# Three of eight chunk pairs of twelve projection blocks by seven block products

## The chip, the cores and the metric

The kernel runs on one core of a Trainium2 chip. Its time is the device time of one execution in microseconds, the median of several runs.

## The reference

The reference is a model of one parallel block (stick-breaking attention and chunked attention with relative positions, a gated feed-forward part) and two more layers with state-space, convolution, latent and memory attention parts, in float32, for 256 tokens of width 2048. What matters here is its first projection, of which the first 6144 columns are q, k and v of both attentions:

```
h = rmsnorm(x, g_mix[i])
proj = h @ w_in[i]          # (256, 2048) @ (2048, 10240)
q_sb, k_sb, v_sb, q_ca, k_ca, v_ca, gate_sb, gate_ca = jnp.split(proj, splits, axis=-1)
```

The kernel multiplies by the gain `g_mix` ahead of the product and by the token's `rstd` behind it.

## The kernel before

**Units.** All weights come as one stream of 919 units. A unit is 256 rows (two chunks of 128) by 512 columns of a weight matrix, 128x1024 float32 in SBUF, 512 KB. A block of the projection is 512 columns, thus 8 units (2048 rows). The tokens are two halves of 128 (`TH`). The stage `win` has 20 blocks; the first twelve (6144 columns) are run in a loop of six pairs of blocks, the other eight in a second loop with the attention beside them.

**Three products for one.** Each operand is split into a high part (`w_hi`, rounded to fp32r by ScalarE, line 1287) and a low part (`w_lo` = raw - `w_hi`, by VectorE, line 1883). The sources stand in SBUF as `x_t` in two parts. `unit` (from line 843) does 2 chunks x 2 halves x 3 products = 12 matmuls of 128x128 by 512 columns: eight with `w_hi` (line 853), then, behind a wait for `lo_ready`, four with `w_lo` (line 859). Its last matmul raises `unit_used`.

**The ring.** `raw`, `w_hi` and `w_lo` have four slots each (`RING`). SyncE's `load` of unit u waits until `w_lo` of unit u - 4 is written (`lo_ready`), and then starts the DMA (line 409). ScalarE's `split` of u waits for the landed load and for `unit_used` of u - 4, VectorE's for ScalarE's. Both run three units ahead of TensorE (`LEAD`): their instruction lists have, at unit k, the split of k + 3.

**The end of a block.** A block sums into two PSUM banks of `acc` (128x512, one for each half of the tokens), two blocks alternate. Behind the eight splits ScalarE waits for the block's last unit and writes `tile` = `acc` x `rstd` (`scale_out`, line 1339), raising `sums_out`. GpSimd (POOL) stores the tile to `d_in` in HBM (`store_tile`, line 447).

**What comes next.** In block 12 the attention begins. POOL, when blocks 0 to 10 are stored, issues the loads of four heads (`load_head`, lines 525 and 528: four DMAs into `qk_b` and one into `v_h` each), then stores block 11. Block 10 holds values of the second attention's heads. VectorE transposes head 0 (line 2021) at unit 0 of block 12, ahead of the `w_lo` of that block's unit 3; TensorE does its scores (lines 930 and 931) ahead of unit 2. The queues run in order. The banks `ps_s`, `ps_y` and `turn` are used by attention and transposes and are idle during the first twelve blocks.

Of the kernel before, what the change touches and what calls it, by code (L numbers as in the profile page):

```python
# [18 lines left out]
UCH = 2  # L19
# [81 lines left out]
def program(nc, io, ctx):  # L101
# [303 lines left out]
    @block.sync
    def _(sp):
        def load(u):
            sp.wait_ge(lo_ready, u.times(1, 1))
            sp.dma_start(raw[:, u.slot, :], stream[bass.ds(u.times(1), 1), :, :].rearrange("a p n -> p (a n)"))\
              .then_inc(raw_landed[u.slot], 16)  # L410

        def load_mem_c(n):
# [24 lines left out]
    def _(pool):  # L437
# [18 lines left out]
        pool.memset(ident[:, :], 0.0).then_inc(zeroed, 1)  # L456
        pool.memset(past[:, :], 0.0).then_inc(zeroed, 1)
        pool.memset(expo[:, :], -0.5).then_inc(zeroed, 1)
        pool.wait_ge(zeroed, 1)
# [1418 lines left out]
    def _(dve):  # L1878
# [995 lines left out]
```

## Time and profile before

| | us |
|---|---|
| median of 3 runs | 2629.84 (2629.19 to 2631.1) |
| the profiled execution | 2629.57 |
| its span | 2628.0 |
| TensorE busy | 2616.2 |
| VectorE busy | 1567.4 |
| ScalarE busy | 1355.2 |
| GpSimd busy | 346.3 |
| DMA | 614.92 MB, 234 GB/s |

The span runs from the first to the last instruction. A matmul's length in the trace contains its way through the array, so that two neighbours overlap; the distance of their starts is what one costs. "PEld" are TensorE's loads of its stationary operand. The releaser of a wait is worked out from semaphore events. The load's landing is the time from its issue to the arrival of its last byte.

### The profile page before, as it was taken

Reading aid. Unit: us, or ns where it says so; the run is one execution under the profiler, and the core shown is the slowest. Engines: PE = TensorE matmul, PEld = TensorE weight load, DVE = VectorE, ACT = ScalarE, POOL = GpSimd, SP = SyncE. Lnnn points to the kernel's source line nnn. Section 1 sums busy time; section 2 is a strip of 40 time slices with the busy share of each in tenths; the row PEclk is TensorE's granted clock in tenths of the full one; section 3 lists DMA queues with packets and bytes.
Section 4 is the critical chain, followed back from the end, with each engine's and each line's share of the span. In section 5 each row is a group of like instructions: output and inputs, shape, how many; then the busy total and the mean of one; then the engine's idle time right before and its main releaser. Section 6 shows DMA issues by size and latency. Waiting matters only on the chain.

```text
span 2628.0 us, 35552 instructions
## 1 busy us (share of the span) xinstructions
PE 2616.2 (100%) x12005; PEld 2171.8 (83%) x12005; DVE 1567.4 (60%) x1830; ACT 1355.2 (52%) x1782; POOL 346.3 (13%) x542
## 2 busy tenths in 40 slices
PE   9999999999999999999999999999999999999998
PEld 7888888888888888888888888888878889888887
DVE  6444456667555555555555575445787855557864
ACT  6544455655444444444444555446667545554443
POOL 2100033211110000000000121001111010123300
PEclk9999999999999999999999999999999999999999
DMA  8876677678866767677766787667788887787875
GB/s 306 311 234 216 219 236 215 213 244 275 254 222 210 224 210 226 211 223 227 219 217 211 256 248 252 207 206 247 241 259 256 249 251 227 224 273 223 225 231 162
DMA packets 176792, 614.92 MB, mean 234 GB/s; under 512 B 23488, under 2 KB 26608, under 8 KB 176432
## 3 DMA queue, kind: packets, MB, share of 16 engines
q1 hardware_dynamic: 133920, 485.55, 56.9%
q0 software_dynamic: 38256, 124.22, 16.2%
q10 hardware_dynamic: 4512, 3.73, 0.5%
q8 instruction: 69, 1.13, 0.2%
q14 instruction: 35, 0.29, 0.0%
HBM read 560.93 MB, written 54.05 MB: 234 GB/s over the span
## 4 chain that ended last, share of the span: by engine, by line
PE 96%; ACT 1%; DVE 1%; DMA 1%; issue 0%; POOLq 0%; POOL 0%; SPq 0%; DVEq 0%; ACTq 0%
PE acc L853 61%; PE acc L859 31%; DMA raw<-stream 1%; ACT w_hi L1287 0%; PE ps_s L1230 0%; PE ps_s L1231 0%; DVE w_lo L1883 0%; DVE cv L2369 0%; ACT dec L1635 0%; PE ps_s L931 0%; PE ps_y L944 0%; PE ps_y L1042 0%; PE ps_s L1023 0%; PE turn L1125 0%; PE turn L1237 0%
## 5 line engine op out<-in xcount | busy, mean ns | idle before, releaser
L1883 DVE TENSOR_TENSOR w_lo<-raw,w_hi 128x1024 fp32r<-128x1024 f32 x918 | 1117.0, 1222 | 872.4 <-ACT w_hi L1287 865.4
L1287 ACT ACTIVATE w_hi<-raw 128x1024 fp32r<-128x1024 f32 x919 | 964.6, 1058 | 929.3 <-PE acc L859 811.9
L853 PE MATMUL acc<-w_hi,x_t_hi 128*128 128x512 f32 (+1 forms) x2400 | 948.7, 395 | 0.0
L853 PE MATMUL acc<-w_hi,x_t_lo 128*128 128x512 f32 (+1 forms) x2400 | 932.7, 389 | 0.0
L859 PE MATMUL acc<-w_lo,x_t_hi 128*128 128x512 f32 (+1 forms) x2400 | 640.1, 388 | 0.5 <-DVE w_lo L1883 0.5
L859 PEld LDWEIGHTS acc<-w_lo,x_t_hi 128*128 128x128 f32 x2400 | 450.2, 188 | 93.5 <-DVE w_lo L1883 1.6
L853 PEld LDWEIGHTS acc<-w_hi,x_t_lo 128*128 128x128 f32 x2400 | 450.8, 188 | 91.5 <-issue 1.9
L853 PEld LDWEIGHTS acc<-w_hi,x_t_hi 128*128 128x128 f32 x2400 | 450.7, 188 | 91.4 <-issue 1.9
L853 PE MATMUL acc<-w_hi,ff_t_hi 128*128 128x512 f32 x352 | 136.9, 389 | 0.0
L853 PE MATMUL acc<-w_hi,ff_t_lo 128*128 128x512 f32 x352 | 136.9, 389 | 0.0
L859 PE MATMUL acc<-w_lo,ff_t_hi 128*128 128x512 f32 x352 | 94.1, 389 | 0.0
L853 PE MATMUL acc<-w_hi,z_t_hi 128*128 128x512 f32 x224 | 87.3, 390 | 0.0
L853 PE MATMUL acc<-w_hi,z_t_lo 128*128 128x512 f32 x224 | 87.2, 389 | 0.0
L853 PEld LDWEIGHTS acc<-w_hi,ff_t_lo 128*128 128x128 f32 x352 | 66.1, 188 | 13.8
L859 PEld LDWEIGHTS acc<-w_lo,ff_t_hi 128*128 128x128 f32 x352 | 66.1, 188 | 13.8
L853 PEld LDWEIGHTS acc<-w_hi,ff_t_hi 128*128 128x128 f32 x352 | 66.0, 188 | 13.7
L447 POOL DMA_DIRECT2D d_x<-tile x16 | 11.6, 726 | 432.5 <-DVE tile L2141 274.7
L859 PE MATMUL acc<-w_lo,z_t_hi 128*128 128x512 f32 x224 | 59.9, 389 | 0.0
L603 POOL DMA_DIRECT2D d_h<-tile x11 | 8.0, 726 | 384.6 <-DVE tile L2166 384.6
L853 PE MATMUL acc<-w_hi,o_t_hi 128*128 128x512 f32 x144 | 56.5, 393 | 0.0
L853 PE MATMUL acc<-w_hi,o_t_lo 128*128 128x512 f32 x144 | 56.1, 389 | 0.0
L853 PE MATMUL acc<-w_hi,lat_t_hi 128*128 128x512 f32 x136 | 55.0, 404 | 0.0
(385 smaller groups left out, 2649.0 us busy)
## 6 DMA issues: line engine op xcount, KB each, us to landing
raw<-stream SPq DMA_DIRECT2D x919, 512.0 KB, 4.3
d_in<-tile POOLq DMA_DIRECT2D x20, 512.0 KB, 3.7
d_ev<-tile POOLq DMA_DIRECT2D x20, 512.0 KB, 4.5
d_x<-tile POOLq DMA_DIRECT2D x16, 512.0 KB, 4.1
r_b<-d_x POOLq DMA_DIRECT2D x64, 128.0 KB, 5.5
xin<-d_x POOLq DMA_DIRECT2D x16, 512.0 KB, 7.7
d_h<-tile POOLq DMA_DIRECT2D x14, 512.0 KB, 5.6
h_b<-d_h POOLq DMA_DIRECT2D x56, 128.0 KB, 4.2
```

The lines of the kernel that those rows point to most:

```text
L447: pool.dma_start(dst[:, :, bass.ds(b.times(NBW), NBW)], tile[slot][:, :, :])\
L603: pool.dma_start(halves(d_h), tile[0][:, :, :]).then_inc(cols_in, 16)
L853: nc.tensor.matmul(out, src[x][:, chunk + c, t * P:(t + 1) * P], w_hi[:, s, w], start=first and c == 0 and x == 0, stop=False)
L859: mm = nc.tensor.matmul(acc[2 * bank + t][:, 0:width], src[0][:, chunk + c, t * P:(t + 1) * P], w_lo[:, s, w], start=False, stop=last and ...
L1287: nc.scalar.activation(w_hi[:, u.slot, :], raw[:, u.slot, :], ACT.Copy).then_inc(hi_ready, 1)
L1883: nc.vector.tensor_tensor(w_lo[:, s, :], raw[:, s, :], w_hi[:, s, :].bitcast(F32), ALU.subtract).then_inc(lo_ready, 1)
```

## The change

The twelve blocks are computed in six pairs of neighbours (two blocks side by side, 1024 columns), interleaved: for each of the eight chunk pairs k first the unit of the one block, then of the other. For k = 1, 3, 5 the two units, seen as a matrix of 2 x 2 blocks (chunk by column block), and the source, seen as 2 x 2 (half of the tokens by chunk), are multiplied in a form of Strassen's (Winograd's variant) with seven products in place of eight, each of three matmuls. Such a step has four units in the ring: the two loaded ones and two that VectorE makes by four sums of 128x512 in the raw slots u+2 and u+3 (`weight_sums`); of the second loaded one only a half is split (`split_second`). ScalarE and VectorE split the made ones like loaded ones. The load of the unit behind a step waits for one `w_lo` more (`later`). A pair has 22 units in the ring, 16 of them loaded (PU, MADE); `PAIR` lists them: 0, 1 plain; 2 to 5 step; 6, 7 plain; 8 to 11 step; 12, 13 plain; 14 to 17 step; 18 to 21 plain.

The products common to several results go to four banks `q`, the rest to four banks `c`; the two sets (`acc` and `ps_s`, `ps_y`, `turn`) change places from pair to pair. Behind the third step ScalarE copies `q[0]` and VectorE adds the others (`drain`, before the `w_lo` of n + 3 at n = 19); at the end of the pair VectorE adds these to `c` (`closing`, for the first block at n = 21, for the second behind it), and ScalarE multiplies the tiles of both blocks by `rstd`. The sums of the source (three times four of 128x128, with their splits) are made beside the last two blocks of the memory stage. Otherwise semaphores are merged (`zeroed`, `bias_ready`), and the stream is put in the new order. From block 12 on the kernel is as before.

```diff
-    ("mem", 4, 8), ("win", 20, 8), ("out", 8, 4), ("mix", 4, 8), ("ffn", 22, 8),
+    ("mem", 4, 8), ("pairs", 12, 11), ("win", 8, 8), ("out", 8, 4), ("mix", 4, 8), ("ffn", 22, 8),
...
+U0["win"] -= 96
+B0["win"] -= 12
+STEPS = (1, 3, 5)
+PAIR = []
+for _k in range(8):
+    PAIR += [("step" if _k in STEPS else "plain", _k, j) for j in range(4 if _k in STEPS else 2)]
+PU = len(PAIR)
+MADE = sum(kind == "step" and j >= 2 for kind, _, j in PAIR)
+STEP_AT = [PAIR.index(("step", k, 0)) for k in STEPS]
+PAIRS_END = U0["pairs"] + 6 * PU
+W_ALL = 2 * len(STEPS) + 5
+W_FIRST = 2 * len(STEPS)
...
+    s_w = place("s_w", [P, len(STEPS), 4, P], F32, WD + 80 * K)
+    s_hi = place("s_hi", [P, len(STEPS), 4, P], F32R, T0 + 4 * K)
+    s_lo = place("s_lo", [P, len(STEPS), 4, P], F32R, T0 + (4 + 2 * len(STEPS)) * K)
+    v_w = place("v_w", [P, 4, NBW], F32, WD)
...
-        def load(u):
-            sp.wait_ge(lo_ready, u.times(1, 1))
-            sp.dma_start(raw[:, u.slot, :], stream[bass.ds(u.times(1), 1), :, :].rearrange("a p n -> p (a n)"))\
+        def load(u, at=None, later=0):
+            sp.wait_ge(lo_ready, u.times(1, 1 + later))
+            sp.dma_start(raw[:, u.slot, :], stream[bass.ds((at or u).times(1), 1), :, :].rearrange("a p n -> p (a n)"))\
               .then_inc(raw_landed[u.slot], 16)
...
-        with sp.Fori(0, N_UNITS // RING - 1) as i:
+        with sp.Fori(0, U0["pairs"] // RING - 1) as i:
             for s in range(RING):
                 load(At(RING + s, i, RING))
-        for u in range(N_UNITS // RING * RING, N_UNITS):
-            load(At(u))
+        with sp.Fori(0, 3) as i:
+            at = U0["pairs"]
+            for n, (kind, _, j) in enumerate(2 * PAIR):
+                if j < 2:
+                    load(At(U0["pairs"] + n, i, 2 * PU), At(at, i, 32), n % PU - 4 in STEP_AT)
+                    at += 1
+        with sp.Fori(0, (N_UNITS - PAIRS_END) // RING) as i:
+            for s in range(RING):
+                load(At(PAIRS_END + s, i, RING), At(PAIRS_END - 6 * MADE + s, i, RING))
+        for u in range(N_UNITS - (N_UNITS - PAIRS_END) % RING, N_UNITS):
+            load(At(u), At(u - 6 * MADE))
...
-        pe.wait_ge(const_ready, 1)
-
-
-        with pe.Fori(0, 6) as i:
-            for b in range(2):
-                pe.wait_ge(sums_out, blk("win", b, i).times(1, 1))
-                for k in range(8):
-                    source(TURN["x"], k)
-                    unit(At(U0["win"] + 8 * b + k, i, 16), x_t, UCH * k, b, k == 0, k == 7)
+        pe.wait_ge(const_ready, 4)
+        own = (ps_s, ps_y, turn[0], turn[1])
+        def x_of(t, chunk):
+            return tuple(h[:, chunk, t * P:(t + 1) * P] for h in x_t)
+        def products(u, todo):
+            pe.wait_ge(hi_ready, u.times(1, 1))
+            for a, half, out, first, _ in todo:
+                w = w_hi[:, u.slot, half * NBW:(half + 1) * NBW]
+                for x in range(2):
+                    nc.tensor.matmul(out[:, :], a[x], w, start=first and x == 0, stop=False)
+            pe.wait_ge(lo_ready, u.times(1, 1 + RING))
+            for a, half, out, _, last in todo:
+                mm = nc.tensor.matmul(out[:, :], a[0], w_lo[:, u.slot, half * NBW:(half + 1) * NBW],
+                                      start=False, stop=last)
+            mm.then_inc(unit_used, 1)
+        def step(u, n, k, c, q):
+            def s_of(j):
+                return s_hi[:, n, j, :], s_lo[:, n, j, :]
+            f, e = n == 0, n == len(STEPS) - 1
+            products(u, [(x_of(0, 2 * k), 0, q[0], f, e), (x_of(0, 2 * k + 1), 1, c[0][0], False, False)])
+            products(u + 1, [(s_of(3), 1, c[1][0], False, False)])
+            products(u + 2, [(s_of(0), 0, q[1], f, e), (s_of(2), 1, q[3], f, e)])
+            products(u + 3, [(s_of(1), 0, q[2], f, e), (x_of(1, 2 * k + 1), 1, c[0][1], False, False)])
+        def plain(u, k, c):
+            products(u, [(x_of(t, 2 * k + h), h, c[t], k == 0 and h == 0, k == 7 and h == 1)
+                         for h in range(2) for t in range(TH)])
+        with pe.Fori(0, 3) as i:
+            for r in range(2):
+                c, q = (own, acc) if r == 0 else (acc, own)
+                c = (c[0:2], c[2:4])
+                pe.wait_ge(w_sum, At(S_SUMS + W_ALL * r, i, 2 * W_ALL).times(1, -2))
+                for n, (kind, k, j) in enumerate(PAIR):
+                    u = At(U0["pairs"] + PU * r + n, i, 2 * PU)
+                    if j == 0:
+                        source(TURN["x"], k)
+                    if kind == "plain":
+                        plain(u, k, c[j])
+                    elif j == 0:
+                        if k == STEPS[0]:
+                            pe.wait_ge(sums_out, B0["mem"] + 3 + 3)
+                            pe.wait_ge(w_sum, At(S_SUMS + W_ALL * r, i, 2 * W_ALL).times(1))
+                        step(u, STEPS.index(k), k, c, q)
...
+        def split_second(u):
+            act.wait_ge(raw_landed[u.slot], u.landed())
+            act.wait_ge(unit_used, u.times(1, 1))
+            nc.scalar.activation(w_hi[:, u.slot, NBW:UW], raw[:, u.slot, NBW:UW], ACT.Copy).then_inc(hi_ready, 1)
...
-        with act.Fori(0, 6) as i:
-            for b in range(2):
-                splits("win", 8, 8 * b, i, 16)
-                scale_out(At(U0["win"] + 8 * b + 7, i, 16), b, At(STORED["win"], i, 1).times(16, 16), 1)
+        with act.Fori(0, 3) as i:
+            for r in range(2):
+                q = acc[0] if r == 0 else ps_s
+                for n in range(PU):
+                    if n == STEP_AT[-1] + 2:
+                        summed(At(U0["pairs"] + PU * r + STEP_AT[-1], i, 2 * PU))
+                        nc.scalar.activation(v_w[:, 0, :], q[:, :], ACT.Copy).then_inc(w_act, 1)
+                    u = At(U0["pairs"] + PU * r + n + LEAD, i, 2 * PU)
+                    kind, _, j = PAIR[(n + LEAD) % PU]
+                    (split_second if (kind, j) == ("step", 1) else split)(u)
+                for b in range(2):
+                    act.wait_ge(w_sum, At(S_SUMS + W_ALL * r + W_ALL - 1 + b, i, 2 * W_ALL).times(1))
+                    for t in range(TH):
+                        last = nc.scalar.activation(tile[b][:, t, :], tile[b][:, t, :], ACT.Copy, scale=rstd[:, 2 + t:3 + t])
+                    last.then_inc(sums_out, 1)
...
+        def weight_sums(u, count):
+            dve.wait_ge(raw_landed[u.slot], u.landed())
+            dve.wait_ge(raw_landed[(u + 1).slot], (u + 1).landed())
+            dve.wait_ge(lo_ready, u.times(1, RING))
+            (b11, b21), (b12, b22), (t1, t3), (t2, t4) = (
+                (raw[:, (u + n).slot, 0:NBW], raw[:, (u + n).slot, NBW:UW]) for n in range(4))
+            nc.vector.tensor_tensor(t1, b12, b11, ALU.subtract).then_inc(w_sum, 1)
+            nc.vector.tensor_tensor(t3, b22, b12, ALU.subtract).then_inc(raw_landed[(u + 2).slot], 16)
+            dve.wait_ge(w_sum, count.times(1, 1))
+            nc.vector.tensor_tensor(t2, t1, b22, ALU.subtract).then_inc(w_sum, 1)
+            dve.wait_ge(w_sum, count.times(1, 2))
+            nc.vector.tensor_tensor(t4, b21, t2, ALU.add).then_inc(raw_landed[(u + 3).slot], 16)
...
+        def drain(u, q, count, copied):
+            summed(u)
+            dve.wait_ge(w_act, copied)
+            nc.vector.tensor_tensor(v_w[:, 2, :], q[2][:, :], v_w[:, 0, :], ALU.add).then_inc(w_sum, 1)
+            dve.wait_ge(w_sum, count.times(1, 1))
+            nc.vector.tensor_tensor(v_w[:, 1, :], q[3][:, :], v_w[:, 2, :], ALU.add).then_inc(w_sum, 1)
+            dve.wait_ge(w_sum, count.times(1, 2))
+            nc.vector.tensor_tensor(v_w[:, 3, :], q[1][:, :], v_w[:, 1, :], ALU.add)
+            nc.vector.tensor_tensor(v_w[:, 2, :], q[1][:, :], v_w[:, 2, :], ALU.add).then_inc(w_sum, 1)
+        def closing(u, c, b, stored, count):
+            summed(u)
+            dve.wait_ge(tile_moved[b], stored)
+            dve.wait_ge(w_sum, count)
+            for t in range(TH):
+                last = nc.vector.tensor_tensor(tile[b][:, t, :], c[2 * b + t][:, :], v_w[:, 2 * b + t, :], ALU.add)
+            last.then_inc(w_sum, 1)
...
-        with dve.Fori(0, 6) as i:
-            for b in range(2):
-                splits("win", 8, 8 * b, i, 16)
+        own = (ps_s, ps_y, turn[0], turn[1])
+        with dve.Fori(0, 3) as i:
+            for r in range(2):
+                c, q = (own, acc) if r == 0 else (acc, own)
+                def at(n):
+                    return At(U0["pairs"] + PU * r + n, i, 2 * PU)
+                def sums(n):
+                    return At(S_SUMS + W_ALL * r + n, i, 2 * W_ALL)
+                stored = At(STORED["win"] + r, i, 2).times(16, 16)
+                for n in range(PU):
+                    if n + LEAD - 1 in STEP_AT:
+                        m = STEP_AT.index(n + LEAD - 1)
+                        weight_sums(at(n + LEAD - 1), sums(2 * m))
+                    if n == STEP_AT[-1] + 5:
+                        drain(at(STEP_AT[-1] + 3), q, sums(W_FIRST), At(S_ACTS + r, i, 2).times(1, 1))
+                    if n == PU - 1:
+                        closing(at(PU - 2), c, 0, stored, sums(W_FIRST + 3).times(1))
+                    kind, _, j = PAIR[(n + LEAD) % PU]
+                    (split_second if (kind, j) == ("step", 1) else split)(at(n + LEAD))
+                closing(at(PU - 1), c, 1, stored, sums(W_FIRST + 3).times(1))
...
-    units = [tiles_of(mem), tiles_of(win),
+    ahead = [16 * p + 8 * b + k for p in range(6) for k in range(8) for b in range(2)]
+    win = tiles_of(win)
+    units = [tiles_of(mem), win[ahead], win[96:],
...
```

## Rows read from the trace of the kernel before

**Rows 1.** The page: span, busy times, granted clock in 40 slices, chain by line.
```profile
span 2628.0 us, 35552 instructions
PE 2616.2 (100%) x12005; PEld 2171.8 (83%) x12005; DVE 1567.4 (60%) x1830; ACT 1355.2 (52%) x1782; POOL 346.3 (13%) x542
...
PEclk9999999999999999999999999999999999999999
...
PE acc L853 61%; PE acc L859 31%; DMA raw<-stream 1%; ACT w_hi L1287 0%; PE ps_s L1230 0%; PE ps_s L1231 0%; DVE w_lo L1883 0%; DVE cv L2369 0%; ACT dec L1635 0%; PE ps_s L931 0%; PE ps_y L944 0%; PE ps_y L1042 0%; PE ps_s L1023 0%; PE turn L1125 0%; PE turn L1237 0%
```

**Rows 2.** Timeline of TensorE, 330 to 372: start, length, engine, line, form.
```profile
353.14 0.39 PE L853 MATMUL acc<-w_hi,x_t_hi 128*128 128x512 f32 x1
...
355.86 0.39 PE L853 MATMUL acc<-w_hi,x_t_hi 128*128 128x512 f32 x1
...
361.30 0.38 PE L930 MATMUL ps_s<-qk_t 128*128 128x128 f32 x2
```

**Rows 3.** Timeline of ScalarE, 330 to 375; in brackets idle time and releaser.
```profile
334.38 1.27 ACT L1339 ACTIVATE tile<-acc,rstd 128x512 f32<-128x512 f32 x2 [1.74 <-PE acc L859]
...
353.34 1.06 ACT L1287 ACTIVATE w_hi<-raw 128x1024 fp32r<-128x1024 f32 x1 [1.66 <-PE acc L859]
356.06 1.27 ACT L1339 ACTIVATE tile<-acc,rstd 128x512 f32<-128x512 f32 x2 [1.66 <-PE acc L859]
```

**Rows 4.** Timeline of VectorE, 340 to 385.
```profile
354.43 1.23 DVE L1883 TENSOR_TENSOR w_lo<-raw,w_hi 128x1024 fp32r<-128x1024 f32 x1 [1.49 <-ACT w_hi L1287]
355.58 0.70 DVE L2021 STREAM_TRANSPOSE qk_t<-qk_b 128x512 f32<-128x512 f32 x1
...
368.38 0.42 DVE L2045 TENSOR_TENSOR_SCAN left<-ones,drop 128x128 f32<-128x128 f32 x1
368.72 0.67 DVE L2047 TENSOR_TENSOR_SCAN left<-ones,drop 128x256 f32<-128x256 f32 x1
369.42 0.56 DVE L2051 TENSOR_TENSOR left<-z_sb,left 128x384 f32<-128x384 f32 x1
```

**Rows 5.** Waits of the load queue, 100 to 300: total us, times, longest.
```profile
SPq L409 <- DVE w_lo L1883: 153.1, 75, 5.5
```

**Rows 6.** Tile raw, 200 to 240: landing of its loads.
```profile
DMA to landing us min/median/max: 4.0/4.3/4.8
```

**Rows 7.** Groups by line and form: busy us, mean ns, idle before.
```profile
L1339 ACT ACTIVATE tile<-acc,rstd 128x512 f32<-128x512 f32 x48 | 30.3, 683 | 29.8 <-PE acc L859 25.6 <-DMA d_mem<-tile 4.2
...
L2141 DVE TENSOR_TENSOR tile<-acc,xin 128x512 f32<-128x512 f32 x16 | 10.3, 686 | 2.7 <-PE acc L859 2.7
...
L2099 DVE TENSOR_TENSOR tile<-part 128x512 f32<-128x512 f32 x8 | 5.2, 687 | 0.1
```

**Rows 8.** Timeline of VectorE, 84 to 104.
```profile
93.14 1.23 DVE L1883 TENSOR_TENSOR w_lo<-raw,w_hi 128x1024 fp32r<-128x1024 f32 x1 [3.53 <-ACT w_hi L1287]
...
100.53 3.50 DVE L1883 TENSOR_TENSOR w_lo<-raw,w_hi 128x1024 fp32r<-128x1024 f32 x3 [2.57 <-ACT w_hi L1287]
```

**Rows 9.** Windows: busy by engine, granted clock, share of DMA engines, GB/s.
```profile
8.00:10.00 2.00, 2.00 (x11) 1.62 (x10) 1.51 (x3) 1.60 (x3) 0.00 (x0) 1.00 1.01 408
118.00:140.00 22.00, 22.00 (x99) 18.22 (x98) 10.94 (x9) 11.32 (x14) 3.44 (x5) 1.00 0.91 322
```

**Rows 10.** Timeline of ScalarE, 60 to 104.
```profile
99.43 2.96 ACT L1287 ACTIVATE w_hi<-raw 128x1024 fp32r<-128x1024 f32 x3 [1.86 <-POOL rstd L482]
```

**Rows 11.** Tile raw, 100 to 300: landing of its loads.
```profile
DMA to landing us min/median/max: 3.1/4.3/10.2
```

**Rows 12.** Timeline of GpSimd, 340 to 385.
```profile
340.55 2.33 POOL L525 DMA_DIRECT2D qk_b<-d_in  x4 [3.89 <-DMA d_in<-tile]
342.88 0.72 POOL L528 DMA_DIRECT2D v_h<-d_in  x1
```

**Rows 13.** DMA issues, 335 to 336.5: KB each, us to landing.
```profile
d_in<-tile POOLq DMA_DIRECT2D x1, 512.0 KB, 4.0
```

**Rows 14.** DMA issues, 342.5 to 343.5.
```profile
v_h<-d_in POOLq DMA_DIRECT2D x1, 128.0 KB, 5.9
```

**Rows 15.** DMA issues, 351 to 352.5.
```profile
v_h<-d_in POOLq DMA_DIRECT2D x1, 128.0 KB, 8.0
```

**Rows 16.** DMA issues, 81 to 85.
```profile
raw<-stream SPq DMA_DIRECT2D x3, 512.0 KB, 8.3
```

More of the change, by code:

```diff
@@ L290, in program @@
     unit_used = sem("unit_used")
+    w_sum = sem("w_sum")
+    w_act = sem("w_act")
     sums_out = sem("sums_out")
@@ L309, in program @@
     rstd_ready = sem("rstd_ready")
-    zeroed = sem("zeroed")
     const_ready = sem("const_ready")
@@ L321, in program @@
     e_built = sem("e_built")
-    bias_in, bias_ready = sem("bias_in"), sem("bias_ready")
+    bias_in = sem("bias_in")
     at_loaded = [sem(f"at_loaded{s}") for s in range(4)]
@@ L400, in written @@
         return b.times(1, 3)
+    S_SUMS = 3 * len(STEPS)
+    S_ACTS = 2 * len(STEPS)
     block = ctx.enter_context(nc.Block())
@@ L455, in _ @@
         pool.dma_start(posi[:, :], io["positions"]).then_inc(tile_moved[0], 16)
[L456 to L459, printed above, removed]
+        pool.memset(ident[:, :], 0.0).then_inc(const_ready, 1)
+        pool.memset(past[:, :], 0.0).then_inc(const_ready, 1)
+        pool.memset(expo[:, :], -0.5).then_inc(const_ready, 1)
+        pool.wait_ge(const_ready, 1)
         pool.affine_select(out=ident[:, :], in_=ident[:, :], compare_op=ALU.not_equal, fill=1.0, base=0,
@@ L472, in _ @@
                            pattern=[[1, P]], channel_multiplier=-1).then_inc(mask_ready, 1)
-        pool.wait_ge(zeroed, 3)
+        pool.wait_ge(const_ready, 4)
         for at in (0, TOK):
@@ L511, in _ @@
         pool.wait_ge(bias_in, 64)
-        pool.memset(bias[0:CHUNK, :, CHUNK:P], NEG).then_inc(bias_ready, 1)
-        pool.memset(bias[0:CHUNK, :, H3 - CHUNK:H3], NEG).then_inc(bias_ready, 1)
+        pool.memset(bias[0:CHUNK, :, CHUNK:P], NEG).then_inc(mask_ready, 1)
+        pool.memset(bias[0:CHUNK, :, H3 - CHUNK:H3], NEG).then_inc(mask_ready, 1)
         din_v = halves(d_in)
@@ L735, in _ @@
         pool.memset(causal[:, :], 0.0).then_inc(mask_ready, 1)
-        pool.wait_ge(mask_ready, 5)
+        pool.wait_ge(mask_ready, 7)
         for at in (0, TOK):
@@ L1380, in beside_mem @@
                 square(xin[n % 2], 8, At(n), 4 + n)
+            if b == 2 and k - 1 in STEPS:
+                n = STEPS.index(k - 1)
+                for c in range(2):
+                    last = nc.scalar.activation(a_w[:, n, c, :], x_c[(k - 1) // 2][:, 2 * ((k - 1) % 2) + c, :], ACT.Copy,
+                                                scale=gain[:, 16 + 2 * (k - 1) + c:17 + 2 * (k - 1) + c])
+                last.then_inc(w_act, 1)
+            if b == 3 and k - 2 in range(len(STEPS)):
+                act.wait_ge(w_sum, 3 * (k - 2) + 3)
+                nc.scalar.activation(s_hi[:, k - 2, :, :].rearrange("p j t -> p (j t)"),
+                                     s_w[:, k - 2, :, :].rearrange("p j t -> p (j t)"), ACT.Copy).then_inc(w_act, 1)
         act.wait_ge(ones_ready, 1)
@@ L1884, in split, with split_second @@
                                     ALU.subtract).then_inc(lo_ready, 1)
+        def split_second(u):
+            dve.wait_ge(hi_ready, u.times(1, 1))
+            s = u.slot
+            nc.vector.tensor_tensor(w_lo[:, s, NBW:UW], raw[:, s, NBW:UW], w_hi[:, s, NBW:UW].bitcast(F32),
+                                    ALU.subtract).then_inc(lo_ready, 1)
+        def weight_sums(u, count):
[10 more added lines that the diff above has]
+            nc.vector.tensor_tensor(t4, b21, t2, ALU.add).then_inc(raw_landed[(u + 3).slot], 16)
@@ new lines, in source_sums @@
+        def source_sums(n):
+            dve.wait_ge(w_act, n + 1)
+            a11, a21, a12 = a_w[:, n, 0, 0:P], a_w[:, n, 0, P:TOK], a_w[:, n, 1, 0:P]
+            a22 = a_w[:, n, 1, P:TOK]
+            s1, s2, s3, s4 = (s_w[:, n, j, :] for j in range(4))
+            nc.vector.tensor_tensor(s1, a21, a22, ALU.add).then_inc(w_sum, 1)
+            nc.vector.tensor_tensor(s3, a11, a21, ALU.subtract)
+            dve.wait_ge(w_sum, 3 * n + 1)
+            nc.vector.tensor_tensor(s2, a11, s1, ALU.subtract).then_inc(w_sum, 1)
+            dve.wait_ge(w_sum, 3 * n + 2)
+            nc.vector.tensor_tensor(s4, a12, s2, ALU.add).then_inc(w_sum, 1)
@@ new lines, in source_low @@
+        def source_low(n):
+            dve.wait_ge(w_act, len(STEPS) + n + 1)
+            hi, lo, src = (x[:, n, :, :].rearrange("p j t -> p (j t)") for x in (s_hi, s_lo, s_w))
+            nc.vector.tensor_tensor(lo, src, hi.bitcast(F32), ALU.subtract)
+        def drain(u, q, count, copied):
[7 more added lines that the diff above has]
+            nc.vector.tensor_tensor(v_w[:, 2, :], q[1][:, :], v_w[:, 2, :], ALU.add).then_inc(w_sum, 1)
@@ L1994, in beside_mem @@
                 x_low(k)
+            if b == 3 and k in range(len(STEPS)):
+                source_sums(k)
+            if b == 3 and k - 3 in range(len(STEPS)):
+                source_low(k - 3)
         for u in range(LEAD):
@@ L2070, in attend @@
                         ALU.subtract).then_inc(at_y_lo, 1)
-        dve.wait_ge(mask_ready, 4)
-        dve.wait_ge(bias_ready, 2)
+        dve.wait_ge(mask_ready, 6)
         with dve.Fori(0, 4) as i:
@@ L2731, in latent_heads @@
                                                 ALU.subtract).then_inc(turn_lo, 1)
-        dve.wait_ge(mask_ready, 7)
+        dve.wait_ge(mask_ready, 9)
         for n in range(4):
```

1 line of the change is left out of this document (added).

## The prediction

> **What bounds the kernel now.** I read the page's busy table and its chain first: TensorE is busy 2616.2 of 2628.0 us, and the chain that ended last is 61% and 31% on the two matmul lines of `unit` [rows 1]. So time changes by matmuls taken out and by stalls put in, and by nothing else. Then the TensorE timeline, for the price of a matmul: a unit of twelve begins at 353.14 and the next at 355.86, 2.72 us or 0.2267 us each [rows 2]. The 96 units of the first twelve projection blocks are 261.4 us by this; they end at 355.86. Then I looked for how far the other engines run ahead. ScalarE writes `w_hi` of the unit three ahead 0.2 us after a unit of PE ended (353.34 behind 353.14, 356.06 behind 355.86), in 1.06 us; VectorE follows 0.03 us later (354.43) with `w_lo` in 1.23 us [rows 2 to 4]. In the steady stage `w_lo` waits for `w_hi`, and the load queue (SP) waits for `w_lo`, 153.1 us over 75 loads [rows 5]: the ring is given back only when VectorE is done, and a load then takes 4.0 to 4.8 us, median 4.3 [rows 6]. That costs nothing now, because PE reaches the unit so loaded four units (10.9 us) on. The change touches exactly this ring.
>
> **What it takes away.** A chunk pair of a block pair is 2 units, 24 matmuls; a step has 7 products of 3 matmuls, 21. Three steps in each of six pairs: 54 matmuls x 0.2267 = -12.2 us [rows 2]. A pair of blocks is then 183 matmuls, 41.5 us of PE, where it had 43.5.
>
> **What it adds to VectorE and ScalarE.** Per pair VectorE has 19 full and 3 half `w_lo` (1.23 and 0.69 us; back to back a full one costs 1.17, by three in 3.50), 12 sums of 128x512 (0.69 us as such an add of two SBUF tiles; 0.62 where it needn't wait for the one before, as a scan of 0.42 is followed after 0.34; 0.03 is between dependent ones), 4 of the drain and 4 of the closing at 0.69 each from PSUM: 22.8 + 2.1 + 7.9 + 5.5 = 38.3 of 41.5 us [rows 4, 7, 8]. It fits, but without room. ScalarE has 19 x 1.06 + 3 x 0.56 + 0.68 + 4 x 0.68 = 25.2 us: room [rows 3, 7]. So neither is the bound by its sum. What decides is the order in time.
>
> **The turnaround of the ring.** A step uses all four raw slots: u and u+1 hold weights, u+2 and u+3 the sums. The load of u+4 goes over slot u, whose second half the last sum reads, so it waits for `w_lo` of u+1 (`later`), which VectorE does after the four sums. Nothing can be ahead. From `w_lo`(u+1) to PE's first matmul of u+4: issue 0.1, landing 4.3, `w_hi` 1.06 with 0.1 before it, 0.05: 5.6 us [rows 3, 6]. PE's work in that time is what follows the `w_lo` wait of u+1: 1 + 6 + 6 matmuls, 2.95 us. If PE is just at that wait, it stalls 5.6 - 2.95 = 2.65 us.
>
> Is VectorE early enough with u+1, or earlier? Steps 1 to 2 and 2 to 3 of a pair are six units apart, and the cycle from one `w_lo`(u+1) to the next is: 0.1 + 4.3 + 0.1 + 1.06 + 0.03 + 1.23 = 6.82 to `w_lo` of the first plain unit; two more `w_lo` at the spacing of landings, 1.3 us each (512 KB at the 408 GB/s of a stretch with full engines): 9.42; four sums, 0.62 + 0.62 + 0.72 + 0.69 = 2.65: 12.07; the half `w_lo` 0.69: 12.76 [rows 4, 7, 9]. PE needs 45 x 0.2267 = 10.20. So the cycle, not PE, sets the pace, 2.56 us late each time, the same 2.6 as the turnaround: PE is indeed just at that wait. PE would be the bound again only with a landing under 4.3 - 2.56 = 1.7 us. The first step of a pair stands behind six plain units and has more room, but VectorE comes to it with drain and closing in its queue. With `w_lo`(18) of a pair at T - 9.7 (T is the pair's end), three more at 1.3 to 1.4, drain 2.8, two `w_lo` 2.4, it begins the closing at T - 0.3, ends its first half at T + 1.0, then `w_lo`(2), closing, four sums and `w_lo`(3): T + 1.0 + 1.2 + 1.35 + 2.65 + 0.69 = T + 6.9. PE's own time at that wait is T + 5.44 + 1.36 + 0.45 = T + 7.25. On time by 0.35, so the turnaround behind it costs 2.65 - 0.35 = 2.3 or, with some slip, the same 2.6. I take 2.6 for each of 18 steps: +46.8 us. In the first pair ScalarE is held by `rstd` to 99.43, 4.9 us behind the pair's start at 355.86 - 261.4 = 94.5 [rows 10]; its `w_hi` of unit 3 then is 100.0, before PE's need: no further term.
>
> Bounds of the 2.6: landing 4.0 or 4.8 (the ends of the row) gives 2.3 or 3.1; if the loads, now in bunches of four, come 1.66 us apart (the 322 GB/s at 0.91 of the engines where other traffic runs too), another 0.36 x 2 in two of three steps [rows 6, 9]. So 2.3 to 3.6 us, 41 to 65 in all. Below lies the shortest landing in 75, 3.1 us [rows 11]: 1.4 each, 25. The stores of both blocks now fall together at the pair's end instead of 21.8 us apart; two of 512 KB are 2.6 us of the engines there, before the loads behind step 1 are issued (T + 7); cost taken 0, bound +1 a pair.
>
> One rule of the Trainium skill would make this cheaper. The row: 15 loads took 4.0 to 4.8 us. The page DMA: Bandwidth & Descriptors, section "Anatomy of one DMA", fits a transfer as some 2.0 us and its bytes over 436 GB/s, 3.2 us for 512 KB (an estimate by that page); by it the stall were 1.55 us and the kernel near 2656. The trace does not agree, and the sum goes by the trace.
>
> **The hand-over to block 12.** The queries' and keys' heads 0 to 3 are loaded from `d_in` once block 10 is stored. Now block 10 ends 21.8 us ahead of block 11: its tile is done at 334.38 + 1.27 = 335.65, POOL is let go by the landed store (4.0 us) at 340.55, 4.90 later, head 0's five DMAs are issued by 343.59, and its `v_h`, issued at 342.88, lands 5.9 later, 348.8: 8.2 us after the first issue [rows 3, 12 to 14]. All that ends before PE asks (361.30, two units into block 12). In pairs, blocks 10 and 11 end together: block 10's tile is done at T + 1.0 + 0.1 + 1.27 = T + 2.4. Then 4.9 + 8.2, the transpose 0.70 and 0.05: T + 16.25, and PE, whose queue is in order, stands at the scores from T + 5.44: +10.8 us, once [rows 2, 4]. VectorE waits for the same head before `w_lo` of block 12's fourth unit, so that is up with the end of this stall (1.23 against 2.7 + 1.8 of matmuls) and adds nothing. Bounds: the tile at T + 0.2 without VectorE's backlog, +8.6; the last heads' landing 8.0 instead of 5.9, +13 [rows 15].
>
> **Costed at nothing.** The small sums and copies of sources in the last two blocks of the memory stage (fifteen instructions of VectorE and nine of ScalarE, none above 0.7 us): VectorE idles there behind late loads, 3.53 us before one `w_lo` [rows 8]; without that cover, 1 us. The loop of three long bodies instead of six: PE's queue covers the turn, as now. Semaphores renamed and merged, masks, stream order (the same bytes in a row): nothing.
>
> **Sum.** -12.2 + 46.8 + 10.8 = +45.4. The profiled execution took 2629.57 us, its span 2628.0; the median of the three runs is 2629.84. 2629.8 + 45.4 = 2675 us.
>
> **Rivals.**
> 1. The landings are short when the queue has been empty (3.1 us): 25 + 10.8 - 12.2 = +24, 2653 us. For it: the minimum is there [rows 11]. Against: in a quiet stage none of 15 is below 4.0 [rows 6]. 0.12.
> 2. The other side: the loads keep up. The mechanism is the slack of PE's cover: if VectorE gets to `w_lo`(u+1) early by over 2.65 us in each step, PE sees no turnaround, and only -12.2 is left: 2617.6, or with the hand-over's stall 2628. It decides from stalls under 0.68 us a step (0.08 with the hand-over's stall). The plain units between steps speak for it, the cycle of 12.76 against 10.20 speaks against it. 0.05, half of it with the hand-over's stall.
> 3. Bunched loads, stores and VectorE's sums disturb each other: the upper bounds together and more, 65 + 13 + 6 - 12 = +72, 2702. For it: three loads issued from 81 to 85 beside other transfers took 8.3 us [rows 16]. 0.08.
> 4. The clock. The granted clock is in its top tenth in each of 40 slices, the level of 2.4 GHz [rows 1]; PE has no idle of microseconds behind its first unit, so no row shows what follows one. If each of the 18 stalls left half of the 45 matmuls behind it at 1.2 GHz, that is 18 x 22.5 x 0.2267 = 92 us more, 2767. The page TensorE: Matmul & The Clock Gate ("HAM oscillation") has this as a failure of kernels that wait for loads in every turn. Against it: PE still works 10.2 of 12.8 us in a cycle. Behind the one spell of 10.8 us, two units at 1.2 GHz would be 5 us. 0.03.
> The change may also compute less than it says; the counts of products say it doesn't.
>
> **How the numbers follow.** Forecast 0.72, rivals 0.12, 0.05, 0.08, 0.03. The likeliest case by its own bounds: 41 + 8.6 - 12.2 = +37 to 65 + 13 - 12.2 = +66, 2667 to 2696. The range takes in most of rival 1 and the edge of 3: 2650 to 2700. No change is within 0.2%, 2624.6 to 2635.1, which is what a measurement can tell. Faster 0.03, within 0.03, slower 0.94.
>
> **What would show it.** In the profile after: 18 idle spells of PE of 2 to 3.5 us, each released by `w_hi` of the first plain unit behind a step, whose ScalarE copy waits for the raw load; a pair 49 to 50 us long instead of 43.5; VectorE busy some 38 us a pair; the median landing near 4.3 still; one PE idle spell of about 11 us at the scores of block 12. It is wrong if PE waits in the steps for `w_lo` (then VectorE's sums are the bound), if the raw loads land in 3 us, or if the granted clock falls.

## The result and the profile after

The changed kernel takes 2674.15 us (median of four runs, 2672.06 to 2676.54) against 2629.53 (four runs, 2629.19 to 2631.1) for the kernel before: ratio 1.0169, 95% interval 1.0151 to 1.0186. It is 44.6 us slower; forecast were 45.4. The sum came out nearer than its terms.

The page of the changed kernel, the lines that answer to [rows 1]:

```profile
span 2670.5 us, 35793 instructions
PE 2620.1 (98%) x11951; PEld 2164.4 (81%) x11951; DVE 1674.7 (63%) x2001; ACT 1393.2 (52%) x1833; POOL 343.9 (13%) x542
...
PE acc L884 54%; PE acc L890 27%; DMA raw<-stream 5%; DVE w_lo L1985 2%; ACT w_hi L1362 1%; DMA d_mem<-tile 1%; DVE raw L2005 0%; DVE w_lo L1992 0%; DVE tile L2044 0%; PE ps_s L1305 0%; PE ps_s L1306 0%; DVE raw L2002 0%; DMA dec<-d_ac 0%; PE turn L1200 0%; PE ps_s L1006 0%
```

There are 54 matmuls fewer, as many as counted, and yet TensorE is busy 4 us longer. Some ran at the lower clock; besides, a matmul ahead of an idle spell counts with its whole length, as nothing overlaps it (368 matmuls at full clock count as 85.4 us busy in this kernel and as 83.0 in one without idle spells, both shown below). The raw loads, 1% of the chain before, are 5% of it now. Who let TensorE go, from its table of waits (total us, times, longest; in the kernel before it is empty from 94 to 400):

```profile
PE acc L957 <- ACT w_hi L1362: 14.1, 9, 2.9
PE ps_s L957 <- ACT w_hi L1362: 12.4, 8, 2.8
PE ps_s L1005 <- DVE qk_t L2206: 5.5, 1, 5.5
PE turn L960 <- DVE w_lo L1992: 2.5, 3, 2.0
PE acc L884 <- ACT tile L1499: 2.3, 1, 2.3
```

The first two rows are 17 waits for `w_hi` of the first plain unit behind a step (of 18 steps; only the third of pair 1 has none); the third is the scores of block 12; the fifth is block 12's first matmul, waiting for block 10's tile. Line 957 is the high products in `products`, line 960 the low ones.

The pairs begin at 95.00, 148.92, 197.47, 245.11, 292.55 and 340.15, and the last ends at 387.19 (starts of their first matmuls in TensorE's timeline). So they last 53.9, 48.6, 47.6, 47.4, 47.6 and 47.0 us, 292.2 in all against 261.1 (94.74 to 355.86 in the trace of before). One cycle of pair 4, in order of time, first VectorE, then ScalarE, then TensorE (start, length, engine, line):

```profile
263.99 0.69 DVE L1992 TENSOR_TENSOR w_lo<-raw,w_hi 128x512 fp32r<-128x512 f32 x1
264.59 2.35 DVE L1985 TENSOR_TENSOR w_lo<-raw,w_hi 128x1024 fp32r<-128x1024 f32 x2
269.15 1.23 DVE L1985 TENSOR_TENSOR w_lo<-raw,w_hi 128x1024 fp32r<-128x1024 f32 x1 [2.20 <-ACT w_hi L1362]
270.61 1.22 DVE L1985 TENSOR_TENSOR w_lo<-raw,w_hi 128x1024 fp32r<-128x1024 f32 x1 [0.24 <-ACT w_hi L1362]
272.34 1.23 DVE L1985 TENSOR_TENSOR w_lo<-raw,w_hi 128x1024 fp32r<-128x1024 f32 x1 [0.51 <-ACT w_hi L1362]
273.48 0.68 DVE L2002 TENSOR_TENSOR raw<-raw 128x512 f32<-128x512 f32 x1
274.09 0.69 DVE L2003 TENSOR_TENSOR raw<-raw 128x512 f32<-128x512 f32 x1
274.69 0.68 DVE L2005 TENSOR_TENSOR raw<-raw 128x512 f32<-128x512 f32 x1
275.48 0.69 DVE L2007 TENSOR_TENSOR raw<-raw 128x512 f32<-128x512 f32 x1
276.08 0.69 DVE L1992 TENSOR_TENSOR w_lo<-raw,w_hi 128x512 fp32r<-128x512 f32 x1
```

```profile
280.38 1.06 ACT L1362 ACTIVATE w_hi<-raw 128x1024 fp32r<-128x1024 f32 x1 [3.04 <-DMA raw<-stream]
```

```profile
279.71 0.39 PE L960 MATMUL acc<-w_lo,x_t_hi 128*128 128x512 f32 x1
281.58 0.47 PE L957 MATMUL acc<-w_hi,x_t_hi 128*128 128x512 f32 x1 [1.49 <-ACT w_hi L1362]
```

From one half `w_lo`, that of u+1, (263.99) to the next (276.08) it is 12.09 us, where TensorE needs 10.20: the cycle of the prediction, with 12.76 forecast. From its end at 276.77 to TensorE's start at 281.58 are 4.8 us, where 5.6 were forecast. The two loads issued then landed in 3.7 us, not 4.3 (over all raw loads from 144 to 340 the median is 4.7, with 3.1 to 6.7). Changed kernel, DMA issues from 276.5 to 277.6: count, size, median landing:

```profile
raw<-stream SPq DMA_DIRECT2D x2, 512.0 KB, 3.7
```

Pair 1 is another matter. The first row is its window, the second six microseconds of it (lengths, then busy times of PE, PEld, DVE, ACT and POOL, the granted clock, the share of the DMA engines, GB/s), and behind them the DMA issues from 116 to 124:

```profile
95.00:148.90 53.90, 47.35 (x184) 36.73 (x183) 36.16 (x42) 24.50 (x28) 6.52 (x9) 0.91 0.68 230
118.00:124.00 6.00, 5.08 (x12) 3.40 (x11) 1.39 (x2) 0.00 (x0) 0.00 (x0) 0.56 1.00 354
```

```profile
raw<-stream SPq DMA_DIRECT2D x4, 512.0 KB, 8.7
bias<-d_skew POOLq DMA_DIRECT2D x1, 1024.0 KB, 8.9
bias<-d_skew POOLq DMA_DIRECT2D x1, 512.0 KB, 5.2
```

The bias table of the second attention is loaded just then. Raw loads took 8.7 us beside it, TensorE idled, and the granted clock was 0.56 of full speed in those six microseconds, for the most part the level of 1.2 GHz. The kernel before has the same loads in its first pair, with landings nearly as long, and no wait of TensorE (before, DMA issues from 110 to 124):

```profile
raw<-stream SPq DMA_DIRECT2D x5, 512.0 KB, 7.6
bias<-d_skew POOLq DMA_DIRECT2D x1, 1024.0 KB, 10.5
```

The hand-over, in TensorE's, GpSimd's and VectorE's timelines of the changed kernel:

```profile
389.69 0.79 PE L884 MATMUL acc<-w_hi,x_t_hi 128*128 128x512 f32 x1 [2.34 <-ACT tile L1499]
...
402.46 0.79 PE L1005 MATMUL ps_s<-qk_t 128*128 128x128 f32 x2 [5.52 <-DVE qk_t L2206]
```

```profile
389.86 0.71 POOL L478 DMA_DIRECT2D d_in<-tile  x1 [43.42 <-ACT tile L1499]
396.45 2.33 POOL L556 DMA_DIRECT2D qk_b<-d_in  x4 [5.89 <-DMA d_in<-tile]
398.78 0.72 POOL L559 DMA_DIRECT2D v_h<-d_in  x1
```

```profile
401.62 0.71 DVE L2206 STREAM_TRANSPOSE qk_t<-qk_b 128x512 f32<-128x512 f32 x1 [11.10 <-DMA v_h<-d_in]
```

Before, the loads of the four heads began at 340.55 and the transpose ran at 355.58, ahead of the end of block 11, 355.86 [rows 4, 12]; now they begin 9.3 us behind the end of pair 6, 387.19. The scores come at 402.46, 15.3 us behind it; before it was 361.30 - 355.86 = 5.44 [rows 2].

### The profile page after: what moved, and what is told of

The parts are those of the page before. It is cut to its first block, busy times and chain, and to the rows that moved or that the text cites. A ratio compares the mean times of both kernels' runs of the same rounds, so it can differ in the third digit from the quotient of the medians.

```text
span 2670.5 us, 35793 instructions
## 1 busy us (share of the span) xinstructions
PE 2620.1 (98%) x11951; PEld 2164.4 (81%) x11951; DVE 1674.7 (63%) x2001; ACT 1393.2 (52%) x1833; POOL 343.9 (13%) x542
## 4 chain that ended last, share of the span: by engine, by line
PE 86%; DMA 6%; DVE 4%; issue 2%; ACT 1%; POOL 0%; DVEq 0%; SPq 0%; POOLq 0%; ACTq 0%
PE acc L884 54%; PE acc L890 27%; DMA raw<-stream 5%; DVE w_lo L1985 2%; ACT w_hi L1362 1%; DMA d_mem<-tile 1%; DVE raw L2005 0%; DVE w_lo L1992 0%; DVE tile L2044 0%; PE ps_s L1305 0%; PE ps_s L1306 0%; DVE raw L2002 0%; DMA dec<-d_ac 0%; PE turn L1200 0%; PE ps_s L1006 0%
## 5 line engine op out<-in xcount | busy, mean ns | idle before, releaser
L1985 DVE TENSOR_TENSOR w_lo<-raw,w_hi 128x1024 fp32r<-128x1024 f32 x936 | 1136.9, 1221 | 791.1 <-ACT w_hi L1362 782.9
L1362 ACT ACTIVATE w_hi<-raw 128x1024 fp32r<-128x1024 f32 x937 | 984.0, 1058 | 925.1 <-PE acc L890 709.8
L884 PE MATMUL acc<-w_hi,x_t_hi 128*128 128x512 f32 (+1 forms) x2016 | 801.6, 398 | 2.3 <-ACT tile L1499 2.3
L884 PE MATMUL acc<-w_hi,x_t_lo 128*128 128x512 f32 (+1 forms) x2016 | 784.9, 389 | 0.0
L890 PE MATMUL acc<-w_lo,x_t_hi 128*128 128x512 f32 (+1 forms) x2016 | 537.5, 388 | 0.5 <-DVE w_lo L1985 0.5
L884 PEld LDWEIGHTS acc<-w_hi,x_t_hi 128*128 128x128 f32 x2016 | 379.8, 188 | 79.8 <-issue 4.7
L884 PEld LDWEIGHTS acc<-w_hi,x_t_lo 128*128 128x128 f32 x2016 | 379.9, 188 | 76.8 <-issue 1.9
L890 PEld LDWEIGHTS acc<-w_lo,x_t_hi 128*128 128x128 f32 x2016 | 378.2, 188 | 78.8 <-DVE w_lo L1985 1.9
L957 PE MATMUL acc<-w_hi,x_t_hi 128*128 128x512 f32 x147 | 57.9, 394 | 14.1 <-ACT w_hi L1362 14.1
L957 PE MATMUL acc<-w_hi,x_t_lo 128*128 128x512 f32 x147 | 57.2, 389 | 0.0
```

The lines of the kernel that those rows point to most:

```text
L884: nc.tensor.matmul(out, src[x][:, chunk + c, t * P:(t + 1) * P], w_hi[:, s, w], start=first and c == 0 and x == 0, stop=False)
L890: mm = nc.tensor.matmul(acc[2 * bank + t][:, 0:width], src[0][:, chunk + c, t * P:(t + 1) * P], w_lo[:, s, w], start=False, stop=last and ...
L957: nc.tensor.matmul(out[:, :], a[x], w, start=first and x == 0, stop=False)
L1362: nc.scalar.activation(w_hi[:, u.slot, :], raw[:, u.slot, :], ACT.Copy).then_inc(hi_ready, 1)
L1985: nc.vector.tensor_tensor(w_lo[:, s, :], raw[:, s, :], w_hi[:, s, :].bitcast(F32), ALU.subtract).then_inc(lo_ready, 1)
```

## The experiments

**Where the loss is: steps or hand-over.**

```diff
-STEPS = (1, 3, 5)
+STEPS = ()          # 16 plain units a pair; no drain, no closing;
+                    # ScalarE: tile[b] = c banks x rstd
```

> All eight chunk pairs plain, no step, no sums, no made units; the pairs of blocks, their stream order and the two sets of banks stay, and ScalarE scales each pair's banks at the pair's end. Hand-over theory: the pairing alone delays the store of block 10 by a block, so TensorE stalls at the tile and at the first head's scores of block 12, and part of what follows runs at the lower clock: +9 to +13 us over the kernel before, 2639 to 2643, pairs 43.5 us each. Rival (all of the loss lies in the steps, the heads' loads find time elsewhere): 2630, within 0.1%. Second rival (interleaving two blocks itself costs): pairs over 44 us, more than 2645.

Measured: 2638.65 against 2628.92, ratio 1.0034 (1.0021 to 1.0046), +9.7 us, at the lower edge of what was expected. Two pairs take 87.04 us, 43.52 each, what two blocks one behind the other took: interleaving costs nothing. TensorE's only wait in this stretch:

```profile
PE ps_s L1005 <- DVE qk_t L2206: 7.2, 1, 7.2
```

So the pairing alone, without a single step, loses nearly 10 us at block 12: the first three units of that block end 18.3 us behind the pairs, where before it was 8.84.

```diff
-    ("pairs", 12, 11), ("win", 8, 8)
+    ("pairs", 10, 11), ("win", 10, 8)     # blocks 10 and 11 as before
```

> Only blocks 0 to 9 in pairs with steps; blocks 10 and 11 one behind the other as in the kernel before. Hand-over theory: no stall at block 12, and one pair less with its net 4 us: 53.9 - 43.5 + 4 x (47.7 - 43.5) = +27 over before, 2657. Rival (the stall at block 12 comes from VectorE's backlog or the loop's end, wherever the pairs end): 2657 + 8 to 12 = 2665 to 2669, with the idle spell at the end of pair 5 instead.

Measured: 2653.84, ratio 1.0091 (1.0074 to 1.0108). The stall at block 12 is gone, and TensorE's work from 340 to 400 is unbroken; the stalls at the steps and the long first pair (53.9) stay. Its span, 2654.0, is 16.5 us shorter than the changed kernel's: the hand-over's 11.9 (worked out below) and 5.0 in the twelve blocks, 287.2 us where it was 292.2, with small differences of 0.4 and 0.8 us ahead of them and behind. Between the medians it is 20 us, three more than expected.

**Why the steps stall: ring or VectorE.**

```diff
+    made = place("made", [P, 2, UW], F32, T0 + 16 * K)
-            (b11, b21), (b12, b22), (t1, t3), (t2, t4) = (four raw slots)
+            (b11, b21), (b12, b22) = (two raw slots)
+            (t1, t3), (t2, t4) = ((made[:, n, 0:NBW], made[:, n, NBW:UW]) for n in range(2))
```

A raw slot is found by the count of loaded units; a load waits for the last `w_lo` or sum that reads the unit four loads before it.

> As the changed kernel, but the sums of the weights are written to 8 KB per partition of their own, and the four raw slots hold loaded units only, so a load can be four loaded units ahead, over a step too. VectorE does exactly the same work. Ring theory: the 17 stalls behind steps go, pairs are 41.5 to 42.5 us, only the hand-over's 12 us and something in pair 1 stay: 2628 to 2638. Rival (VectorE's sums and splits, 38 of 41.5 us, are the bound, in their order): pairs stay at 46 us or more, 2660 to 2674, and TensorE waits for w_lo inside the steps.

Measured: 2626.76 against 2628.92, ratio 0.9993 (0.9983 to 1.0002), 47 us faster than the changed kernel and 1 us under the range expected. The pairs: 43.1, then 41.48 each, TensorE's own time for 183 matmuls (41.49). Two pairs of this kernel and, below, nearly two of the changed one (245 to 340):

```profile
221.00:304.00 83.00, 83.00 (x368) 68.73 (x367) 73.72 (x85) 49.06 (x55) 2.86 (x4) 1.00 0.67 227
```

```profile
245.00:340.00 95.00, 85.40 (x368) 67.83 (x367) 73.18 (x84) 49.68 (x54) 2.85 (x4) 1.00 0.57 199
```

The same 368 matmuls, the same 73 to 74 us of VectorE; 83 us in the one, 95 in the other. VectorE at 89% busy is no bound. What differs is where the sums lie, and so when a load may start. TensorE's waits here, from 94 to 400:

```profile
PE ps_s L1024 <- DVE qk_t L2244: 5.4, 1, 5.4
PE ps_s L976 <- ACT w_hi L1381: 0.7, 1, 0.7
PE turn L979 <- DVE w_lo L2027: 0.4, 1, 0.4
PE acc L903 <- ACT tile L1527: 0.3, 1, 0.3
```

The hand-over's stall is still there, but the hand-over costs 8.0 us here and not 12 (the third unit of block 12 ends 16.8 us behind the pairs, less 8.84): the wait for block 10's tile is 0.3 us. Pair 1 carries the bias loads here too and takes 43.1 us, not 53.9. Both edits together:

```diff
+    made = place(...)               # as in the last experiment
+    ("pairs", 10, 11), ("win", 10, 8)   # as in the one before
```

> Both: sums in a place of their own, five pairs, blocks 10 and 11 one behind the other. Ring and hand-over theory: 45 matmuls less and nothing lost, 2629.5 - 10.2 = 2619 to 2623. Rival (VectorE's load bounds the steps): above 2640.

Measured: 2620.7, ratio 0.9966 (0.9954 to 0.9979), in the range expected. Two waits of TensorE in pair 1, 1.3 us, are all that is left.

**Turnaround or cycle.** In the changed kernel, with its sums in the raw slots:

```diff
-            nc.vector.tensor_tensor(t1, b12, b11, ALU.subtract)
+            nc.vector.tensor_tensor(t1[:, 0:32], b12[:, 0:32], b11[:, 0:32], ALU.subtract)
             ... (likewise t3, t2, t4)
```

> The changed kernel with its four sums of the weights cut from 512 to 32 columns each (the rest of the made units is whatever lies there, so steps compute something else); loads, slots and waits stay. Cycle theory (the loop load, first w_lo, two more, four sums, half w_lo sets the pace of 12 us where TensorE needs 10.2): without 2.2 us of sums it is about 9.8 us, under TensorE's, VectorE gets ahead and the stalls nearly go: 2642 to 2652. Rival (a fixed latency of the load against what TensorE has left, whenever w_lo of u+1 comes): the 1.6 us a step stay, above 2668.

Measured: 2648.62, ratio 1.0080 (1.0064 to 1.0095). From pair 3 on the pairs take 42.6 to 43.5 us. TensorE's waits from 94 to 400:

```profile
PE ps_s L957 <- ACT w_hi L1362: 7.1, 4, 4.1
PE ps_s L1005 <- DVE qk_t L2206: 6.9, 1, 6.9
PE acc L957 <- ACT w_hi L1362: 5.7, 3, 3.3
PE acc L884 <- ACT tile L1499: 2.8, 1, 2.8
```

Seven waits for `w_hi` are left of 17. In pairs 3 to 6 they stand only behind the first step, to which VectorE comes from drain and closing; the second and third steps are 10.2 us apart, TensorE's own time. The latency of the load alone would have left them all. It is the loop of load, splits and sums that is too long, and the sums are a part of it.

**Pair 1.** The chain of DMAs for the bias is left out:

```diff
-        pool.dma_start(d_e[:, 0:H3], e_rows[:, :]) ... d_skew ... bias (two loads)
+        pool.memset(bias[:, :, :], 0.0).then_inc(bias_in, 16)
```

> The changed kernel with the bias table set to zero by one memset on GpSimd in place of the chain of small DMAs (through d_e and d_skew) that runs during pair 1; the second attention then lacks its bias. Theory (pair 1 takes 53.9 us and not 47.6 because those DMAs hold up the raw loads and the longer idle spells lower the clock): pair 1 falls to 47.5 to 49.5, 2668 to 2670. Rival (pair 1 is long because ScalarE starts it behind rstd): under 1.5 us, 2672.5 to 2674.

Measured: 2666.97, ratio 1.0146 (1.0131 to 1.0162), 7 us faster than the changed kernel, a little more than expected. Pair 1 took 46.6 us, at full clock, 7.3 us less than in the changed kernel:

```profile
94.60:141.20 46.60, 42.98 (x185) 33.88 (x184) 35.58 (x41) 24.51 (x27) 5.95 (x6) 1.00 0.57 198
```

Here the theory of the contention holds, and the start behind `rstd` costs nothing that shows. Between the spans it is 6.0 us: the other five pairs, in which nothing was changed, took 240.6 us where it was 238.3, so a microsecond or two a pair is not to be read closely.

**The hand-over mended.** The order of the pairs is changed, so that what block 12's first heads need is stored a pair earlier:

```diff
+ORDER = (0, 2, 3, 4, 5, 1)      # blocks 2 and 3 last
-        load_head x 4 behind the store of block 10
+        load_head x 4 behind the store of the fifth pair
```

The split sums of the source move by 2 KB, so that head 1's buffer is free.

> Sums in a place of their own, all six pairs with steps, and the pair of blocks 2 and 3 (queries and keys of heads 4 to 7) computed last, so that blocks 10, 0, 4, 6 are stored during it and the first four heads are loaded ahead of block 12. Theory: no stall at steps nor at the hand-over, 54 matmuls gone: 2628.9 - 12.2 = 2616.7, with the 2 us that are left in pair 1 2617 to 2620, faster than the 2620.7 of five pairs. Rival (the end of pair 6 itself costs, where TensorE waits for block 10's tile): 2621 to 2624.

Measured: 2618.66 against 2629.17, ratio 0.9962 (0.9949 to 0.9976). With all 54 matmuls less (12.2 us) it is 10.5 us faster than the kernel before, the lowest median of all versions. Its waits of TensorE from 94 to 400:

```profile
PE turn L981 <- DVE w_lo L2029: 1.2, 1, 1.2
PE acc L905 <- ACT tile L1529: 0.3, 1, 0.3
```

Its 2 us against five pairs (2620.7) can't be told from nothing: the intervals of the two ratios overlap.

With the order alone, and the sums in the raw slots:

```diff
-    made = place(...)               # sums in the raw slots again
+ORDER = (0, 2, 3, 4, 5, 1)
```

> The changed kernel with its sums in the raw slots as they were, but with the pair of blocks 2 and 3 computed last and the first heads loaded during it. Hand-over theory: only the stall at the scores of block 12 goes, with the lower clock behind it; the wait of TensorE for block 10's tile and the steps' stalls stay: 2674 - 8 to 10 = 2663 to 2667. Rival (the two losses overlap, so that taking one away gives nothing while the other stays): above 2670.

Measured: 2666.10, ratio 1.0144 (1.0127 to 1.0161), 8 us faster than the changed kernel: the two losses add (between sums in the raw slots and in their own place lie 47.4 us with either order). The wait for block 10's tile stays (2.3 us), and the hand-over costs 2.6 us where it was 11.9. But pair 6 takes 50.4 us where it was 47.0: the loads of the first four heads, 348.74 to 360.87, now run beside it. In the version with the sums in their own place these loads run beside pair 6 too, and it takes 41.9.

**How far VectorE goes.**

```diff
-STEPS = (1, 3, 5)
+STEPS = (1, 3, 4, 5)
```

> As e7_own_order with a fourth step (chunk pairs 1, 3, 4 and 5): 180 matmuls a pair, 40.8 us of TensorE. VectorE then has 20 full and 4 half w_lo, 16 sums, drain and closing: 20 x 1.2 + 4 x 0.69 + 16 x 0.66 + 5.5 = 42.8 us. Theory (VectorE becomes the bound): pairs of 42.5 to 44 us with waits for w_lo in the third and fourth step, 2622 to 2633, no faster than three steps. Rival (the short forms of VectorE overlap enough): pairs of 40.8, 2614 to 2616.

Measured: 2631.38, ratio 1.0009 (0.9999 to 1.0018). Pairs take 43.23 us, with waits where they were expected:

```profile
PE turn L981 <- DVE w_lo L2029: 5.5, 5, 1.9
PE acc L981 <- DVE w_lo L2029: 5.4, 6, 1.5
```

```profile
221.00:304.00 83.00, 79.42 (x347) 64.17 (x346) 78.02 (x94) 49.95 (x57) 2.86 (x4) 1.00 0.61 217
```

VectorE is at 94%, and its work for a pair, 42.8 us by the sum made beforehand, is more than TensorE's 40.8; so it is probably the bound here. The fourth step saves 0.7 us of TensorE a pair and loses 2.4 in the waits for `w_lo`. A fourth step that isn't next to others was not tried, so what the row of three steps (3, 4, 5) adds to this is open.

## Why the prediction was right

*54 matmuls, -12.2 us.* Right: 12005 became 11951 in the page, and 183 matmuls take 41.48 us where nothing holds them up.

*The ring's turnaround, 18 x 2.6 = +46.8.* The mechanism was right, and the runs show it: with the loads free to run ahead the stalls are gone at the same work of VectorE (with six pairs and with five); with the sums shortened they go at the second and third steps. That the size was near is in part luck, two errors of opposite sign. In the five pairs behind the first the loss is 238.3 - 5 x 41.5 = 30.8 us, 2.05 a step: a load issued into an empty queue landed in 3.7 us, where I took the 4.3 of the steady stage [rows 6]. In pair 1 it is 53.9 - 41.5 = 12.4 where 7.8 was forecast. Together 43.2. The signs named beforehand came in kind and not in size: 17 waits as described, but of 1.1 to 1.8 us behind most steps instead of 2 to 3.5 (the rest of the 2.05 lies in short waits for `w_lo` of u+1 and in the ends of matmuls that nothing overlaps), and pairs of 47 to 48.6 us instead of 49 to 50.

*Pair 1, "no further term".* Wrong, by 7 us. I had looked at `rstd` and not at what the queues carry in that pair. The bias chain was without cost before, though loads took 7.6 us beside it, since they had 10.9 us until they were needed; the ring without slack pays for it. In the prediction, rival 3 had the contention, but put it in the stores.

*The hand-over, +10.8.* Measured +11.9, from 387.19 to the end of block 12's third unit, 407.92 (20.7 us, before 8.84). The sum had the right total from the wrong parts. TensorE stood at the scores for only 5.7 us, from T + 9.6 and not T + 5.4 on: first it waited 2.5 us for block 10's tile (by the distance of starts; the row says 2.3, since it counts the last matmul's whole length), and then a unit took 1.6 us more at the lower clock (granted 0.63 from 390 to 394). I had the tile ready at T + 2.4, as it was, but used this for the store alone and let block 12 begin at T, though its first matmul waits for that tile. Behind the stall the scores and a unit took another 2.1 us at the lower clock (0.50 from 402 to 406). The transpose began at T + 14.4, forecast T + 15.5, again by two errors: from the tile to the first load of a head were 6.9 us instead of 4.9, and from there to the transpose 5.2 instead of 8.2.

*VectorE and ScalarE not the bound.* Right for three steps (89% busy and no stall); the same sum for four steps gives 42.8, and 43.2 were measured.

*The clock.* Rival 4 did not come as a whole. The middle pairs, with idle spells of 1.3 to 1.8 us, kept the full clock; it fell in pair 1, to 0.91 as a mean, which is at most 0.09 x 53.9 = 4.9 us of work with a part of it hidden in stalls, and in block 12 behind the waits of 2.3 and 5.5 us. What the clock costs was only read from these windows and not tried by itself.

*The sum.* -12.2 + 43.2 + 11.9 = 42.9, with 0.3 us more ahead of the pairs (they begin at 95.00, before at 94.74) and 0.7 less behind block 12's third unit: 42.5 in the spans. Between the medians it is 44.6, since the profiled execution of the changed kernel, 2672.06, is the fastest of its four. The forecast, 45.4, was too high by 3.6 for the steps and too low by 1.1 for the hand-over. (The 261.4 us that I gave for the 96 units before were 261.1; nothing rests on it.)

The losses of hand-over and steps add, as the runs with one of them show. The wait for block 10's tile is 0.3 us where the sums have a place of their own and 2.3 to 2.8 where they lie in the raw slots, and the traces say why: VectorE comes late to the closing. TensorE had ended the unit that the closing waits for at 384.47 in the changed kernel; VectorE came to it at 386.91, without a gap from the drain on, which began at 381.99, 5.2 us ahead of the pair's end. In their own place the sums let the drain begin 8.1 us ahead of it, at 336.99, and the closing waits for TensorE (VectorE's timelines, changed kernel and the version with the sums in a place of their own):

```profile
386.91 1.28 DVE L2044 TENSOR_TENSOR tile<-acc,v_w 128x512 f32<-128x512 f32 x2
```

```profile
342.79 1.29 DVE L2079 TENSOR_TENSOR tile<-acc,v_w 128x512 f32<-128x512 f32 x2 [0.57 <-PE acc L979]
```

No run moved drain or closing alone.

## What to carry to other kernels

When work between load and use is put into the buffers that the loads need, write down the cycle from one release of a buffer to the next (load, splits, sums, release) and set it against the time of the bound engine: busy shares say nothing of it. A count of loads ahead that is comfortable in a steady stage hides other traffic too, and when it goes, transfers that were free begin to cost. When the order of results changes, look who reads the last of them first.

## What the runs showed of the hardware that I had not expected

The lower clock came behind spells much shorter than the hand-over's: in the changed kernel it followed idle spells of 1.2 and 2.0 us with two matmuls between them (granted clock 0.56 from 118 to 124), while single spells of 1.3 to 1.8 us with some 10 us of work behind each left it at 1.00 from 245 to 340. The length of one spell doesn't decide it: 3.0 us ahead of 162.23 left 1.00 (162 to 166), and 2.3 us ahead of block 12 was followed by 0.63 (390 to 394), but the same wait of 2.3 us in the version with the order alone by 1.00 (392 to 396). The same loads of 512 KB landed in 3.7 us by twos in an empty queue, in 4.3 in the steady stage and in 8.7 beside the two loads of the bias table, 1.5 MB.
